# Two mixed-attention layers and an expert stage on one core: the order of the weight and modulation loads, and where a layer's loads begin

## What is computed

```python
for l in range(DEPTH):                      # DEPTH = 2
    h = _rms_norm(x, norm_g[l])
    proj = jnp.einsum('bsd,dn->bsn', h, w_in[l])
    # three kinds of attention on slices of proj:
    #   A: 6 heads, decay from a cumulative log-sigmoid of the column a_f
    #   B: 6 heads, q and k/v from low-rank pieces with RMS norms, w_uq, w_ukv, rope
    #   C: 4 heads, difference of two softmaxes; scores + rel_bias[bucket], then the chunk mask
    mixed = jnp.concatenate([a_out, b_out, c_out], axis=-1)   # each times silu of its gate
    x = x + jnp.einsum('bsm,md->bsd', mixed, w_out[l])
```

## Time and profile before

| | |
|---|---|
| median of three executions | 2557.09 us |
| the profiled execution | 2550.7 us |
| its span | 2548.9 us |
| mean granted TensorE clock | 0.967 of full speed |
| busy: TensorE | 2269.9 us (89%) |
| busy: VectorE | 1414.1 us (55%) |
| busy: ScalarE | 726.7 us (29%) |
| first block | about 0 to 1114 us of the span |
| second attention | about 1114 to 1560 us |
| experts | the rest |

### The profile page before, as it was taken

How to read it: one execution, slowest core, us unless ns; L and a number is a source line. 1 busy time by engine, 2 the same in 40 slices (tenths; PEclk the granted TensorE clock), 3 DMA queues, 4 the chain that set the end, 5 groups by cost and what they waited for, 6 DMA issues and landing times. The chain is left out here.

```text
span 2548.9 us, 37257 instructions
## 1 busy us (share of the span) xinstructions
PE 2269.9 (89%) x14757; PEld 1673.6 (66%) x14757; DVE 1414.1 (55%) x2015; ACT 726.7 (29%) x1347; POOL 44.2 (2%) x66
## 2 busy tenths in 40 slices
PE   6999999889999998969989896999888888888886
PEld 5789988768799987758778675544444444444442
DVE  3778798765778898854544555333333333333334
ACT  2444444333443445344544433000000000000001
POOL 0100000000100000011000000000000000000000
PEclk8999999997999999989999997999999999999998
DMA  5877766764877666864434325999999999999997
GB/s 195 307 286 290 282 245 256 268 239 189 337 285 291 263 258 238 327 230 146 141 125 149 116 98 203 401 422 422 422 422 422 422 422 422 422 422 422 422 422 318
DMA packets 109410, 762.55 MB, mean 299 GB/s; under 512 B 12369, under 2 KB 16241, under 8 KB 17521
## 3 DMA queue, kind: packets, MB, share of 16 engines
q1 hardware_dynamic: 109152, 760.21, 75.3%
q10 hardware_dynamic: 144, 0.79, 0.1%
HBM read 758.00 MB, written 2.95 MB: 299 GB/s over the span
## 5 line engine op out<-in xcount | busy, mean ns | idle before, releaser
L2260 PE MATMUL b_ps<-s_raw,s_window 128*64 128x256 f32 x4096 | 460.9, 382 | 58.8 <-DVE x_tokens L2486 39.2
L2260 PEld LDWEIGHTS b_ps<-s_raw,s_window 128*64 128x64 f32 x4096 | 295.4, 137 | 235.9 <-issue 72.6
L1141 DVE TENSOR_TENSOR s_w_tail<-s_raw,s_w_head 128x1024 fp32r<-128x1024 f32 x292 | 345.0, 1223 | 86.1 <-ACT s_w_head L742 85.8
L927 PE MATMUL b_ps<-s_h_head,s_w_head 128*128 128x256 f32 x1184 | 343.3, 290 | 13.8 <-DVE s_w_tail L1141 13.8
L742 ACT ACTIVATE s_w_head<-s_raw 128x1024 fp32r<-128x1024 f32 x292 | 292.5, 1050 | 188.3 <-DMA s_raw<-in_w 176.4
L928 PE MATMUL b_ps<-s_h_tail,s_w_head 128*128 128x256 f32 x1184 | 336.2, 284 | 0.0
L929 PE MATMUL b_ps<-s_h_head,s_w_tail 128*128 128x256 f32 x1184 | 336.1, 284 | 0.0
L1218 DVE SCALAR_TENSOR_TENSOR s_ada_acc<-s_raw,s_c_col,s_ada_acc 128x2048 f32<-128x2048 f32 x120 | 282.3, 2353 | 0.0
L2280 PE MATMUL b_ps<-s_raw,s_diag 128*64 128x512 f32 x1024 | 238.0, 600 | 39.5 <-DMA s_raw<-in_w_down 24.3
L927 PEld LDWEIGHTS b_ps<-s_h_head,s_w_head 128*128 128x128 f32 x1184 | 228.0, 193 | 29.2 <-DVE s_w_tail L1141 17.5
L928 PEld LDWEIGHTS b_ps<-s_h_tail,s_w_head 128*128 128x128 f32 x1184 | 228.3, 193 | 0.1
(11 more groups left out here) (340 smaller groups left out, 3174.2 us busy)
## 6 DMA issues: line engine op xcount, KB each, us to landing
s_raw<-in_w SPq DMA_DIRECT2D x198, 1024.0 KB, 5.0
s_raw<-in_w_ada SPq DMA_DIRECT2D x128, 1024.0 KB, 7.2
s_raw<-in_w_gate SPq DMA_DIRECT2D x128, 1024.0 KB, 24.1
s_raw<-in_w_up SPq DMA_DIRECT2D x128, 1024.0 KB, 26.5
s_raw<-in_w_down SPq DMA_DIRECT2D x128, 1024.0 KB, 26.6
x_tokens<-in_x SPq DMA_DIRECT2D x1, 2048.0 KB, 7.7
s_rel<-in_rel SPq DMA_DIRECT2D x1, 2048.0 KB, 12.2
s_raw<-mod_rows SPq DMA_DIRECT2D x2, 1024.0 KB, 12.3
```

The source lines that it names most:

```text
L927: pe.matmul(out, head, m_head, start=first, stop=False, skip_group_check=True)
L1141: dve.tensor_tensor(w_tail[:, i % SPLITS, cols], raw[:, slot["w", i], cols], w_head[:, i % SPLITS, cols].bitcast(F32), ALU.subtract)\
L2260: ins = pe.matmul(psum[64 * h:64 * h + 64, c // 4, 0:T], window[:, 4 * (c % 4) + k, :], raw[:, c, k * 512 + h * T:k * 512 + h * T + T], st ...
```

## The change

`stream` is one list over both layers, numbered by a global piece number g from 0 to 145, and in it piece g + 1 of the weights stands ahead of the ada piece that follows piece g: w0, w1, a0, w2, a1, w3, a2. The ring, its depth and what a load waits for stay. The split of piece g + 1 at the step of piece g goes on over the layer's end, so that the first piece of the second layer is split at the last step of the first, and its load and the four behind it wait for nothing but their slots. The parameters of the second layer are loaded from ScalarE's queue after its own wait for `x_done`. The third load of parameters and the wait for it are gone. The bias is loaded and masked once.

```diff
-    stream = []
-    for i in range(n_pieces):
-        stream.append(("w", i))
-        if ada_after(i) is not None:
-            stream.append(("ada", ada_after(i)))
+    total_pieces = DEPTH * n_pieces
+    stream = [("w", g) for g in range(AHEAD)]
+    for g in range(total_pieces):
+        if g + AHEAD < total_pieces:
+            stream.append(("w", g + AHEAD))
+        a = ada_after(g % n_pieces)
+        if a is not None:
+            stream.append(("ada", g // n_pieces * ADA_PIECES + a))
...
-        load_parameters(0)
-        for l in range(DEPTH):
-            for n, (what, i) in enumerate(stream):
-                if n >= RAW:
-
-                    before, m = stream[n - RAW]
-                    if before == "w":
-                        sp.wait_ge(sem["tail_split"], at("tail_split", (m, 1), l))
-                    else:
-                        sp.wait_ge(sem["ada_done"], at("ada_done", m, l))
-                src, count = (d["w1"], n_pieces) if what == "w" else (d["w_ada"], ADA_PIECES)
-                sp.dma_start(raw[:, n % RAW, :], src[l * count + i]).then_inc(sem[f"raw{n % RAW}"], 16)
-                if n == 4 * RAW:
-                    load_bias()
-
-            sp.wait_ge(sem["tail_split"], end("tail_split", l))
-            sp.wait_ge(sem["ada_done"], end("ada_done", l))
-
-            x_done(sp, l)
-            load_parameters(l + 1)
-        sp.wait_ge(sem["par"], 16 * (DEPTH + 1))
+        sp.dma_start(par[:, :], d["par"][0]).then_inc(sem["par"], 16)
+        for n, (what, g) in enumerate(stream):
+            if n >= RAW:
+
+                before, m = stream[n - RAW]
+                if before == "w":
+                    sp.wait_ge(sem["tail_split"], at("tail_split", (m % n_pieces, 1), m // n_pieces))
+                else:
+                    sp.wait_ge(sem["ada_done"], at("ada_done", m % ADA_PIECES, m // ADA_PIECES))
+            src = d["w1"] if what == "w" else d["w_ada"]
+            sp.dma_start(raw[:, n % RAW, :], src[g]).then_inc(sem[f"raw{n % RAW}"], 16)
+            if n == 4 * RAW:
+                load_bias()
...
+            if l:
+                continue
             pool.wait_ge(sem["consts"], 16 * CONST_LOADS)
-            pool.wait_ge(sem["rel_in"], l * 64 + 64)
+            pool.wait_ge(sem["rel_in"], 64)
...
         for l in range(DEPTH):
             chain = Chain(act, sem["act_chain"], 0, l, ACT_LINKS_1)
-            split_head(0, l)
+            if l == 0:
+                split_head(0)
...
                     i, what = s[1], s[2]
-                    for n in range(1 if i == 0 else AHEAD, AHEAD + 1):
-                        if i + n < n_pieces:
-                            split_head(i + n, l)
+                    g = l * n_pieces + i
+                    for n in range(1 if g == 0 else AHEAD, AHEAD + 1):
+                        if g + n < total_pieces:
+                            split_head(g + n)
...
             x_done(act, l)
+            if l + 1 < DEPTH:
+                act.dma_start(par[:, :], d["par"][l + 1]).then_inc(sem["par"], 16)
```

More of the change, by code:

```diff
@@ L587, in piece_used, with half_split_before @@
             full(eng, last, l)
[L589 to L591 removed]
+    def half_split_before(eng, g, part):
+        if g >= SPLITS:
+            l, i = divmod(g - SPLITS, n_pieces)
             if part:
[L593 removed]
+                piece_used(eng, i, l)
             else:
[L595 removed]
+                eng.wait_ge(sem["half_used"], at("half_used", i, l))
     def freed(eng, event, l):
@@ L734, in _, with split_head @@
         act.dma_start(rel_dram, rel_rows).then_inc(sem["rel_out"], 16)
-        def split_head(i, l):
-            ring = slot["w", i]
-            act.wait_ge(sem[f"raw{ring}"], at(f"raw{ring}", ("w", i), l, 16))
+        def split_head(g):
+            ring = slot["w", g]
+            act.wait_ge(sem[f"raw{ring}"], at(f"raw{ring}", ("w", g), 0, 16))
             for part in range(2):
-                half_split_before(act, i, part, l)
+                half_split_before(act, g, part)
                 cols = slice(part * HALF, (part + 1) * HALF)
-                act.activation(w_head[:, i % SPLITS, cols], raw[:, ring, cols], ACT.Copy)\
+                act.activation(w_head[:, g % SPLITS, cols], raw[:, ring, cols], ACT.Copy)\
                    .then_inc(sem["head_split"], 1)
@@ L947, in _ @@
                     pe.wait_ge(sem["tail_split"], at("tail_split", (i, 0), l))
-                    wh, wt = w_head[:, i % SPLITS, :], w_tail[:, i % SPLITS, :]
+                    g = l * n_pieces + i
+                    wh, wt = w_head[:, g % SPLITS, :], w_tail[:, g % SPLITS, :]
                     if what in ("tok", "out"):
@@ L1134, in _, with split_tail @@
         dve.wait_ge(sem["setup_dve"], 4)
-        def split_tail(i, l):
+        def split_tail(g):
+            l, i = divmod(g, n_pieces)
             for part in range(2):
                 dve.wait_ge(sem["head_split"], at("head_split", (i, part), l))
-                half_split_before(dve, i, part, l)
+                half_split_before(dve, g, part)
                 cols = slice(part * HALF, (part + 1) * HALF)
-                dve.tensor_tensor(w_tail[:, i % SPLITS, cols], raw[:, slot["w", i], cols],
-                                  w_head[:, i % SPLITS, cols].bitcast(F32), ALU.subtract)\
+                dve.tensor_tensor(w_tail[:, g % SPLITS, cols], raw[:, slot["w", g], cols],
+                                  w_head[:, g % SPLITS, cols].bitcast(F32), ALU.subtract)\
                    .then_inc(sem["tail_split"], 1)
@@ L1186, in _ @@
                     i, what = s[1], s[2]
-                    for n in range(1 if i == 0 else AHEAD, AHEAD + 1):
-                        if i + n < n_pieces:
-                            split_tail(i + n, l)
+                    g = l * n_pieces + i
+                    for n in range(1 if g == 0 else AHEAD, AHEAD + 1):
+                        if g + n < total_pieces:
+                            split_tail(g + n)
                     if what == "out" and s[4] == 3:
@@ L1208, in _ @@
                     j, k = i // 16, i % 16
-                    ring = slot["ada", i]
-                    dve.wait_ge(sem[f"raw{ring}"], at(f"raw{ring}", ("ada", i), l, 16))
+                    piece = ("ada", l * ADA_PIECES + i)
+                    ring = slot[piece]
+                    dve.wait_ge(sem[f"raw{ring}"], at(f"raw{ring}", piece, 0, 16))
                     if k == 0:
@@ L1273, in _ @@
                     if s[1:] == ("C", 0, 0):
-                        dve.wait_ge(sem["bias"], l + 1)
+                        dve.wait_ge(sem["bias"], 1)
                     ps = full(dve, s, l)
```

5 lines of the change are left out of this document (2 added, 3 removed).

## The result

| | before | after |
|---|---|---|
| median, us (lowest to highest) | 2554.26 (2548.79 to 2561.8), 4 runs | 2528.28 (2526.09 to 2530.63), 4 runs |
| ratio, 95% interval | 1 | 0.990 [0.9876, 0.9923] |
| profiled execution, us | 2550.7 | 2526.09 |
| its span, mean granted clock | 2548.9, 0.967 | 2524.3, 0.968 |

The changed kernel is faster by 26.0 us by the medians and by 24.6 us by the spans. The sum had said 18.1. Of the 10.7 us between the forecast (2539 us) and the measurement, 7.9 are this shortfall, and 2.8 come from the kernel before, whose median was 2557.09 us over three runs and is 2554.26 over four.

What follows compares the result with a forecast made beforehand. TensorE was taken to bound the first block and weight DMA the expert stage. Gains of 10.3 + 4.8 + 3.0 = 18.1 us from the 2557.09 us median gave 2539 us, range 2531 to 2547 us (2529 to 2553 with two rivals).

Steps and rivals of the forecast that it cites:

- Part A: First block: loading weights one piece earlier removes TensorE's 14 waits for tail splits with late loads, 10.3 us.
- five stretches that I picked: First-block stretches where late loads make tail splits late: 14 TensorE waits, 10.3 us of 40.2 us in 34.
- a full VectorE: Claimed cause of the other 20 first-block TensorE waits, 29.9 us, mostly in or shortly behind feature stretches; they stay.
- Part B: Layer's end: weights split early, parameters landing 2.48 us after ScalarE's issue, TensorE starts 4.8 us sooner.
- Part C: First block's end: without the unread third parameter load, the next block's first issue comes 3.0 us sooner.
- Part D: Second layer: dropping the second bias mask saves GpSimd 8.05 us and SP four issues, but gains 0.
- The ada pieces: First block: their loads are released one tail split (2.36 us) later, yet VectorE waits for none.
- First rival: First block: DMA rate binds, not lead, so the load order gives 0 and time is 2549.3 us; chance 0.11.
- Second rival: First block: VectorE lacks room, so half the load-order gain is lost and time is 2544.2 us; chance 0.10.
- Third rival: Shifted TensorE waits bring more half-clock falls, 2.6 us each; all 13 would give 2573 us; chance 0.06.

Runs made afterwards that it cites:

- from the other side: The changed kernel with the old order w0, a0, w1, a1 put back in its stream over both layers: 2547.76 us, ratio 0.9975.
- four slots: The changed kernel with 4 slots instead of 5 in the first block's ring: 2527.89 us, ratio 0.990.
- three slots: The changed kernel with 3 slots instead of 5 in the first block's ring: 2548.06 us, ratio 0.9973.
- the third load: The changed kernel with the third parameter load and SP's wait for it put back at the first block's end: 2531.17 us, ratio 0.9911.
- the bias twice: The changed kernel with the four bias loads and four masks put back in the second layer: 2527.87 us, ratio 0.9897.
- the gates: The kernel with four slots, with each gate's sigmoid moved from VectorE to ScalarE as logarithm and exponential: 2511.44 us, ratio 0.9836.
- the order alone: The kernel before with only each layer's load order changed (w0, w1, a0, w2, a1): 2536.98 us, ratio 0.9932.

## Why the prediction was right in its direction and wrong in its size

| term | forecast, us | the traces, us | timed, us |
|---|---|---|---|
| A, order of the loads | 10.3 | 19.3 | 17.2 alone, 19.5 from the other side |
| B, the layer's end | 4.8 | 3.3 (5.5 with a quick landing) | 6.4 for B, C and D together |
| C, the third load | 3.0 | 3.1 (1.9 with the load put back) | 2.9 |
| D, the bias | 0 | 0 | -0.4 |
| sum | 18.1 | 25.7 | 26.0 |

**Part A failed in its size.** The step "in five stretches that I picked (14 waits, ... = 10.3 us)" summed the right stretches on the wrong rows. Its two conclusions stand: the late loads' waits went (the stretches of 6.2, 7.3, 5.2 and 5.4 us show 1.7, 0, 1.7 and 0), and the waits that it put down to a full VectorE stayed. There are 20 of them on the weight loads' rows (37.2 us) and 18 on the matmul rows (30.9 us), where it had counted 20 (29.9 us). But 24 late ones went and not 14. Of the ten more, eight do not show on the matmul rows at all and two lie outside the stretch that it picked at 110 us. And a weight load's row gives about 0.4 us more of a stall than its matmul row. The sign that the prediction had named for itself, matmul rows that fall from 40.2 to about 30 us, came true (30.9) and could not show the error, as it was read on the same rows. The bounds of 0 and 40.2 us held the true 19.3. The range did not: it took in the cases below 10.3 us, and above them only the clock and the spread.

**Part B was long by 1.5 us in this execution, and short by 0.7 in most others.** The load was issued 0.79 us behind the start of the last x sum, just as SP had done (566.79 - 566.00), not 0.7 us later: ScalarE's queue issued it at 550.19, while the last squares were still running. This made the forecast too small. But in the profiled execution the load landed after 4.77 us (554.96 - 550.19) and not 2.48, which made it too large. Six other versions load `par` from ScalarE's queue too. In five of them (four slots, three slots, the third load, the bias twice, the gates) VectorE waited 2.6 to 2.7 us for it, and from the last x sum to TensorE's next matmul it took 4.6 to 4.7 us. There Part B is worth 10.19 - 4.7 = 5.5 us, and the forecast's 2.48 us of landing was right (547.93 - 545.39 = 2.54 us with the gates on ScalarE). With the old order VectorE waited 4.0 us. What decides between quick and slow landing stays open.

**Part C and Part D held.** C came out at 3.1 us by the profiled execution and at 1.9 to 2.9 with the load put back, and nothing of D can be measured.

**The ada pieces** paid nothing, as forecast: in the changed kernel VectorE waits for none of them. With three slots it does:

```profile
DVE s_ada_acc L1222 <- DMA s_raw<-in_w_ada: 5.0, 6, 2.3
```

**First rival, the rate: fell.** If it bound, the waits would have stayed; the order alone took them away. One of its signs did come: in 620:700 a load of weights takes 7.6 us to land, where it took 6.5. But the loads are issued early enough to bear it. The changed kernel's windows below (columns as in the earlier trace rows) answer to the two of the earlier trace rows, shifted by its lead of 16.6 us at the first layer's end and 20 us behind it. A shorter one follows:

```profile
477.40:549.40 72.00, 69.71 (x310) 55.96 (x308) 60.36 (x46) 31.61 (x41) 0.00 (x0) 1.00 0.90 348
620.00:700.00 80.00, 78.66 (x419) 66.27 (x418) 58.38 (x55) 36.25 (x54) 1.58 (x4) 1.00 0.85 333
...
1028.00:1038.00 10.00, 10.00 (x46) 8.29 (x45) 8.69 (x7) 5.54 (x9) 0.00 (x0) 1.00 1.01 424
```

In the first it moves 348 GB/s instead of 260. In the second it moves a little less than before, 333 instead of 346, and yet TensorE starts 419 matmuls in 80 us instead of 394: not the rate held it back there, but when the loads were issued. In the third, the first block draws 424 GB/s for 10 us and loses nothing by it. The Trainium skill, in "HBM Reference" (Specifications), says that a core streaming alone reaches about 425 GB/s, and that 358 GB/s is its share when both cores of a pair stream. The trace agrees with 422 and 424 GB/s; the rule that the prediction weighed was the one for the other case.

**Second rival, half of A passes to VectorE: fell.** The waits that stay are those that were there for another reason, and the order alone gave 17.2 us, not 5.

**Third rival, the clock: it nearly cancels.** The falls moved, as it said, but not all one way. The changed kernel has the wait of the earlier trace rows too, on TensorE's timeline:

```profile
461.82 0.50 PE L925 MATMUL b_ps<-s_w_head,s_low_head 128*128 128x512 f32 x1 [3.46 <-DVE s_w_tail L1141]
```

It comes out of it at full clock, with 25 matmuls in the 5 us that hold 17 in the earlier trace rows. The same wait in its second layer (995.90 us, 3.46 us) did not stay at full clock: 21 matmuls at 0.85 from 2 us behind it. Below stand the window from 2 us behind the first of them, and the first 93 us of the second block:

```profile
463.84:468.84 5.00, 5.00 (x25) 4.17 (x24) 4.12 (x5) 2.12 (x2) 0.00 (x0) 1.00 1.01 346
...
1087.00:1180.00 93.00, 73.75 (x516) 68.33 (x516) 46.79 (x87) 46.27 (x86) 15.99 (x22) 0.87 0.60 219
```

At the last x sum of the first layer the changed kernel was 566.00 - 549.40 = 16.6 us ahead, where the waits of that layer give 30.4 - 18.6 = 11.8 us: some 4.8 us are left for the clock. The version with four slots supports this. Its row of waits for that layer is the same (18.6 us in 10), but behind its wait of 3.45 us the clock fell, and its last x sum came at 555.25, only 10.8 us ahead. The stretch 400:500 of the changed kernel and of that version:

```profile
400.00:500.00 100.00, 88.71 (x559) 77.61 (x559) 85.14 (x127) 46.27 (x80) 0.00 (x0) 1.00 0.73 269
...
400.00:500.00 100.00, 88.73 (x546) 77.33 (x544) 82.50 (x123) 42.87 (x77) 0.00 (x0) 0.95 0.69 255
```

At the last x sum of the second layer the changed kernel was 1109.76 - 1085.10 = 24.7 us ahead. Of the 8.1 us that came between, Part B is 3.3 and this layer 4.8, where its waits give 26.2 - 18.6 = 7.6: 2.8 us are given back. In these 7.6 us is the wait that grew:

```profile
1017.86 0.50 PE L927 MATMUL b_ps<-s_w_head,s_low_head 128*128 128x512 f32 x1 [1.89 <-DVE s_w_tail L1141]
...
995.90 0.72 PE L925 MATMUL b_ps<-s_w_head,s_low_head 128*128 128x512 f32 x1 [3.46 <-DVE s_w_tail L1141]
```

The first is of the kernel before and the second is the same wait in the changed one. In the kernel before, the clock had fallen ahead of it (0.66 in 1008:1013). TensorE came to it later and waited 1.6 us less for the same busy VectorE. So a fall of the clock ahead of such a wait is in part paid back by the wait. With Part C the changed kernel was 1114.60 - 1086.81 = 27.8 us ahead at the next block's first issue, and 24.6 at the end. The second block's clock tells where at least a part of that went: 0.87, where the same window before (1114.80:1207.80) has 0.91. What all this leaves is about a microsecond or two, which is why the span's 24.6 lies so near the terms' 25.7. That this is so near is in part luck: the gains and losses of the clock were 2 to 5 us each. Why the clock falls behind one wait and not behind its like stays open.

## What to carry to other kernels

Read TensorE's stalls on the rows of its weight loads: matmul rows overlap and hide the first tenths of each stall, and short ones then go missing from the sum (10 of 44 in the kernel before). For a ring of loads compare the lead of each load (from its release to its due time) with its landing: here a lead about as long as the landing lost some 19 us, half a round more won all of it back, and another half round on top added nothing. When a wait goes, ask which is next: at the layer's end it was the weights, then the parameters, then GpSimd's `rstd`.

## What the hardware showed beyond what was expected

- A DMA that stands behind ScalarE's activation in its program was issued 0.06 us after that activation had begun (550.19 against 550.13), 0.57 us before it ended. The load did not wait for the activation ahead of it to finish; nothing in the program makes it wait.
- The parameter load of 191.5 KB, with the ring's loads in flight only for its first half microsecond, was usable 4.77 us after its issue; in other kernels with the same load there, VectorE's wait for it was 2.6 to 4.0 us instead of 4.87. The DMA had moved most of it at once and then went on at 27 GB/s for about 2 us. Its cause was not looked into. The rates of 548 to 560 us in 40 slices show it (the changed kernel's DMA view):

```profile
GB/s 82 328 410 437 382 410 410 410 191 0 61 92 288 222 32 27 27 27 27 5 26 10 0 0 0 0 0 0 0 0 55 0 0 0 0 0 0 0 0 0
```

- VectorE is slower while GpSimd masks: beside the four masks of 128x256, an ada step took 2.83 us and not 2.34, in the kernel before (117.24 and 664.57 us), in the changed one (111.96 and 118.07) and with the bias masked twice (643.87 and 649.98).
- The spread between a kernel's runs went with its loads' lead: 9 to 20 us in the kernel before, 20 with the old order and 14 with three slots, and 1.5 to 4.5 in the changed kernel, with the order alone and with four slots. The first three have 9 to 23 runs and the last three 4 to 6, which makes part of the difference. Two others with the new order spread over 9 and 10 us, so the lead is not all of it.
